# RWKV keys and scan preparation as one block, with the second direction in buffers of its own

## What is computed

```
    def decay(w0, wl, w2):
        logw = -jax.nn.softplus(-(w0 + jnp.tanh(wl) @ w2)) - 0.5
        return jnp.exp(-jnp.exp(logw))
...
    w = jnp.stack([decay(w0_f, wl_f, w2_f), decay(w0_b, wl_b, w2_b)])
    a = jax.nn.sigmoid(jnp.stack([a0_f + al_f @ a2_f, a0_b + al_b @ a2_b]))
    g = jax.nn.sigmoid(gl) @ g2
    kk = heads(k * k_k)
    kk = kk / jnp.maximum(jnp.sqrt(jnp.sum(kk * kk, axis=-1, keepdims=True)), 1e-12)
    k_dir = k * (1.0 + (a - 1.0) * k_a)
    b = kk * heads(a)
```

## Time and profile before

| what | value |
|---|---|
| median of 3 runs | 2814.98 us |
| the three runs | 2815.46, 2814.98, 2808.55 us |
| the profiled execution, its own time | 2809.21 us |
| its span | 2807.4 us |
| keys block, by the timeline | 241.3 to 256.3 us |
| preparation block | 256.6 to 314.2 us |
| first matmul of the scan | 314.50 us |

### The profile page before, as it was taken

One profiled execution on the slowest core, in us unless ns is written; L12 is line 12 of the kernel. 1 busy time (PEld: TensorE's weight loads), 2 busy tenths in 40 slices (PEclk: granted clock), 3 DMA queues, 4 the chain that ended last, 5 costly groups with the idle time before them and its releaser, 6 DMA issues. The chain is left out here.

```text
span 2807.4 us, 42506 instructions
## 1 busy us (share of the span) xinstructions
PE 2462.6 (88%) x18560; PEld 1513.1 (54%) x18560; DVE 1257.8 (45%) x2118; ACT 592.2 (21%) x861; POOL 153.0 (5%) x112
## 2 busy tenths in 40 slices
PE   8977499978999999899777899898989779989887
PEld 6864499956544555388235644343437464434333
DVE  6776766656322332377567611121128741112113
ACT  4343311123111111153501311010012431101001
POOL 0000000013000000020110300000000030000000
PEclk9987599988999999999778999999999889999999
DMA  6560133143999999632110779999972157999996
GB/s 224 185 212 12 54 101 94 57 183 137 417 416 415 418 416 417 259 104 90 39 45 20 289 297 427 428 427 428 427 275 75 62 209 310 427 426 428 427 427 255
DMA packets 121890, 727.04 MB, mean 259 GB/s; under 512 B 12038, under 2 KB 65542, under 8 KB 84679
## 3 DMA queue, kind: packets, MB, share of 16 engines
q1 hardware_dynamic: 92200, 693.82, 61.0%
q10 hardware_dynamic: 29536, 30.93, 3.3%
HBM read 722.63 MB, written 2.10 MB: 258 GB/s over the span
## 5 line engine op out<-in xcount | busy, mean ns | idle before, releaser
L2080 PE MATMUL ps<-s_ring,s_c_XG 128*64 128x512 f32 x2016 | 471.6, 617 | 76.6 <-DMA s_ring<-in_exp_w 62.2
L2080 PEld LDWEIGHTS ps<-s_ring,s_c_XG 128*64 128x64 f32 x2016 | 158.8, 141 | 373.6 <-issue 342.4
L2194 DVE TENSOR_TENSOR s_c_hid<-ps,s_c_sil 128x512 f32<-128x512 f32 x32 | 34.3, 1072 | 507.9 <-PE ps L2080 507.9
L2121 PE MATMUL ps<-s_ring,s_c_hidT 128*64 128x512 f32 x1024 | 223.3, 594 | 0.0
L2080 PE MATMUL ps<-s_ring,s_m_XG 128*64 128x512 f32 x1024 | 222.9, 593 | 0.0
L2080 PEld LDWEIGHTS ps<-s_ring,s_m_XG 128*64 128x64 f32 x1024 | 72.8, 137 | 142.7 <-issue 141.6
L2121 PEld LDWEIGHTS ps<-s_ring,s_c_hidT 128*64 128x64 f32 x1024 | 72.2, 137 | 137.2 <-issue 136.8
L371 PE MATMUL ps<-s_src_part,s_w_hi_at 128*128 128x512 f32 x384 | 124.3, 406 | 0.6 <-DVE s_src_part L1589 0.6
L2206 DVE SCALAR_TENSOR_TENSOR s_c_Y_lo<-ps,s_c_w_slot,s_c_Y_hi 128x512 fp32r<-128x512 f32 x32 | 22.5, 746 | 211.5 <-ACT s_c_Y_hi L2163 211.5
L2121 PE MATMUL ps<-s_ring,s_m_hidT 128*64 128x512 f32 x512 | 113.4, 595 | 0.0
L371 PE MATMUL ps<-s_h_part,s_w_hi 128*128 128x512 f32 x336 | 104.0, 391 | 1.7 <-DVE s_w_lo L349 1.6
(11 more groups left out here) (630 smaller groups left out, 4414.2 us busy)
## 6 DMA issues: line engine op xcount, KB each, us to landing
s_ring<-in_exp_w SPq DMA_DIRECT2D x190, 2048.0 KB, 17.3
s_ring<-in_moe_w_gate SPq DMA_DIRECT2D x32, 2048.0 KB, 12.1
s_ring<-in_moe_w_up SPq DMA_DIRECT2D x32, 2048.0 KB, 14.8
s_ring<-in_moe_w_down SPq DMA_DIRECT2D x32, 2048.0 KB, 12.2
s_mod_w_at<-in_vectors SPq DMA_DIRECT2D x64, 512.0 KB, 4.3
s_mod_w<-in_vectors SPq DMA_DIRECT2D x48, 512.0 KB, 4.6
s_w_raw<-in_w_in ACTq DMA_DIRECT2D x13, 1024.0 KB, 7.2
s_w_raw_at<-in_w_in ACTq DMA_DIRECT2D x8, 1024.0 KB, 5.0
```

The lines of the kernel that those rows point to most:

```text
L2080: last = nc.tensor.matmul(ps[x * SLOTS:(x + 1) * SLOTS, bank + fh, :], XG[:, k, c0:c0 + SLOTS], columns(w[x], at), start=(k == 0), stop=(k ...
L2121: last = nc.tensor.matmul(ps[rows, DOWN + half, :], hidT[:, f, rows], columns(w[x], at), start=(f == 0), stop=(f == nj - 1))
L2194: nc.vector.tensor_tensor(hid_out[:, fh * per:(fh + 1) * per, :], ps[:, UP + fh, :].rearrange("s (p j) -> s p j", j=nj), sil[:, fh * 512:( ...
```

## The change

Both functions go, and one takes their place, with one block: `rwkv_inputs`. The scan's buffers are allocated before it, because it borrows from them: the squares lie in the backward half of the scan's `k` (`sq = kt[:, 1]`), the backward sigmoids in `spare` (the first four tiles of `mix`, which hold GLA's work no longer and RWKV's output not yet), the backward running sum in `v_back`, the backward `a_` in the backward half of `q`. `ex` is still shared by both directions. Each step has a semaphore count of its own (`Since`).

```diff
-        def rwkv_keys(proj, kk, w2, a2, g2, lnk):
...
-        def rwkv_prepare(proj, kk, w2, a2, kd_sum, bufs, reset):
+        def rwkv_inputs(proj, kk, w2, a2, g2, kd_sum, bufs, spare, reset):
...
+            sq = kt[:, 1]
...
+                sgs, ccs, as_, kds = (sg, spare), (cc, v_back), (a_, qt[:, 1]), (kd_sum, kd2)
...
                     @block.tensor
...
+                        for c in range(CT):
+                            head_sums(c)
+                        pe.wait_ge(*here.at(64))
+                        pe.wait_ge(*tanh_done.at(1))
+                        for c in range(CT):
+                            low_w(0, c)
+                        for c in range(CT):
+                            pe.wait_ge(*sig_done.at(c + 1))
+                            low_a(0, c, 4 + c)
+                        pe.wait_ge(*inverted.at(1))
+                        for c in range(CT):
+                            r = slice(32 * c, 32 * c + 32)
+                            nc.tensor.matmul(ps[:, c, :], spread[r, :], sq[r, 1, :], start=True, stop=True).then_inc(*spreaded.up())
+                        for c in range(CT):
+                            pe.wait_ge(*sig_done.at(CT + c + 1))
+                            low_w(1, c)
+                        for c in range(CT):
+                            pe.wait_ge(*scaled_keys.at(c + 1))
+                            low_a(1, c, c)
...
                     @block.scalar
...
+                        def decays(d):
+                            act.wait_ge(*scanned.at(d + 1))
+                            if d:
+                                act.wait_ge(*ex_read.at(1))
...
+                        nc.scalar.activation(proj[:, 12, :], proj[:, 12, :], ACT.Tanh).then_inc(*tanh_done.up())
+                        act.wait_ge(*summed.at(CT))
+                        nc.scalar.activation(sq[:, 0, :], ps[:, 0, :], ACT.Sqrt).then_inc(*rooted.up())
+                        sigmoids(0, 0)
+                        sigmoids(0, 1)
+                        nc.scalar.activation(proj[:, 14, :], proj[:, 14, :], ACT.Sigmoid)
+                        gains(0)
+                        sigmoids(1, 0)
+                        sigmoids(1, 1)
+                        decays(0)
+                        gains(1)
+                        decays(1)
+                        act.wait_ge(*exped.at(4 + TOT))
+                        act.wait_ge(*decayed.at(2))
+                        nc.scalar.activation(v_back[:, :, ::-1], v_[:, :, :], ACT.Copy)
...
                     @block.vector
...
+                        V.reciprocal(sq[:, 1, :], sq[:, 0, :]).then_inc(*inverted.up())
+                        scan(0)
+                        less_own(0)
+                        for c in range(CT):
+                            dve.wait_ge(*spreaded.at(c + 1))
+                            V.tensor_tensor(kk[:, c, :], kk[:, c, :], ps[:, c, :], ALU.mult).then_inc(*scaled_keys.up())
+                        keys(0)
+                        scan(1)
+                        dve.wait_ge(*scaled_keys.at(CT))
+                        gated(0)
+                        products(0)
+                        less_own(1)
+                        keys(1)
+                        gated(1)
+                        products(1)
+                        vlink(V.tensor_tensor(flat(kd_sum), flat(kd_sum), flat(kd2), ALU.add))
...
-                    rwkv_keys(proj, kk, w2, a2, g2, None)
...
-                        rwkv_prepare(proj, kk, w2, a2, kd_sum, bufs, masks["reset"])
+                        rwkv_inputs(proj, kk, w2, a2, g2, kd_sum, bufs, mix[:, 0:CT, :], masks["reset"])
```

More of the change, by code:

```diff
@@ L765, in rwkv_prepare, with _ @@
                 keep = sbuf(st, "rw_keep", [P, CT])
-                m0, a0, v0 = mm_done.n, act_out.n, dve_out.n
-                PER_ACT, PER_DVE = 2 * CT + 6, 4
+                sgs, ccs, as_, kds = (sg, spare), (cc, v_back), (a_, qt[:, 1]), (kd_sum, kd2)
+                EX, SG, CC, TOT = 1, 2, 3, 4
                 with nc.Block() as block:
+                    @block.sync
+                    def _(sp):
+                        for to, name in ((w2[0:64, :], "rw_w2_f"), (w2[64:128, :], "rw_w2_b"), (a2[0:64, :], "rw_a2_f"), (a2[64:128, :], "rw_a2_b")):
+                            sp.dma_start(to, A[name]).then_inc(*here.up(16))
+                        sp.dma_start(g2[:], A["rw_g2"]).then_inc(*gate_here.up(16))
+                        sp.wait_ge(*here.at(64))
+                        sp.wait_ge(*gate_here.at(16))
@@ L769, in _, with head_sums, low_w @@
                     @block.tensor
                     def _(pe):
-                        for d in range(2):
+                        def head_sums(c):
+                            pe.wait_ge(*squared.at(c + 1))
+                            nc.tensor.matmul(ps[32 * c:32 * c + 32, 0, :], head_ones[:, 0:P:4], sq[:, c, :], start=True, stop=True).then_inc(*summed.up())
+                        def low_w(d, c):
                             rows = slice(64 * d, 64 * d + 64)
-                            for j in range(2 * CT):
-                                if d == 1:
-                                    pe.wait_ge(act_out.sem, a0 + j + 1)
-                                c, w, x = j % CT, (w2, a2)[j // CT], proj[rows, 12 + j // CT, :]
-                                nc.tensor.matmul(ps[:, j, :], w[rows, c * P:(c + 1) * P], x, start=True, stop=True).then_inc(*mm_done.up())
+                            nc.tensor.matmul(ps[:, 4 + c, :], w2[rows, c * P:(c + 1) * P], proj[rows, 12, :], start=True, stop=True).then_inc(*low_done.up())
@@ new lines, in low_a @@
+                        def low_a(d, c, bank):
+                            rows = slice(64 * d, 64 * d + 64)
+                            nc.tensor.matmul(ps[:, bank, :], a2[rows, c * P:(c + 1) * P], proj[rows, 13, :], start=True, stop=True).then_inc(*low_done.up())
+                        for c in range(CT):
[4 more added lines that the diff above has]
+                            low_w(0, c)
@@ new lines, in sigmoids, with gains @@
+                        def sigmoids(d, which):
+                            for c in range(CT):
+                                n = (2 * d + which) * CT + c
+                                bank = c if d and which else 4 + c
+                                act.wait_ge(*low_done.at(n + 1))
+                                nc.scalar.activation((sgs, as_)[which][d][:, c, :], ps[:, bank, :], ACT.Sigmoid, bias=vcol((w0_at, a0_at)[which][d], c)).then_inc(*sig_done.up())
+                        def gains(d):
+                            act.wait_ge(*kept.at(1))
+                            act.wait_ge(*sig_done.at((2 * d + 2) * CT))
+                            for c in range(CT):
+                                ins = nc.scalar.activation(kds[d][:, c, :], as_[d][:, c, :], ACT.Identity, bias=keep[:, c:c + 1], scale=vcol("rw_k_a", c))
+                            ins.then_inc(*kd_done.up())
@@ L810, in _, with scan @@
                         V = nc.vector
[L811 to L822 removed]
+                        def scan(d):
@@ new lines, in _ @@
+                        for c in range(CT):
+                            vlink(V.tensor_scalar(kk[:, c, :], k_[:, c, :], vcol("rw_k_k", c), None, ALU.mult))
+                            V.tensor_tensor(sq[:, c, :], kk[:, c, :], kk[:, c, :], ALU.mult).then_inc(*squared.up())
+                        V.tensor_scalar(keep[:], vcol("rw_k_a", 0, CT), -1.0, 1.0, ALU.mult, ALU.add).then_inc(*kept.up())
+                        dve.wait_ge(*rooted.at(1))
+                        vlink(V.tensor_scalar(sq[:, 0, :], sq[:, 0, :], 1e-12, None, ALU.max))
```

129 lines of the change are left out of this document (35 added, 94 removed).

## The result

The changed kernel takes 2794.13 us (median of 7 runs, 2791.45 to 2800.88); before took 2807.24 (7 runs, 2805.41 to 2815.46). The ratio is 0.9942, 95% interval 0.9928 to 0.9956: 0.58% less, 16 us, between 12 and 20; the two medians themselves lie 13.1 us apart (0.47%), so the size of the saving is known to a few us only. All ratios here leave out executions in the chip's slower state (one of e1's ten, 2970.66 us, and one of before beside it, 5045.3 us). The profiled execution has a span of 2792.3 us against 2807.4, 15.1 less. The prediction said 2798 within 2791 to 2808.

What follows compares the result with a forecast made beforehand. DVE was taken to bound the 73 us between GLA and the scan: 13.3 us of waits, plus 0.3 for `keep`, minus 0.3 for new waits, plus 0.2 for gaps, 13.5. 2812.0 less 13.5 gave 2798, range 2791 to 2808.

Steps and rivals of the forecast that it cites:

- How the numbers follow: Whole kernel: 13.5 us saved, taken from the level of before, gives 2798; this forecast had chance 0.79.
- the level of before: Whole kernel's time before the change: 2812.0 us, the middle of the two groups among three runs.
- What bounds: Between GLA and the scan: DVE is the fullest engine, busy 57.01 of 73.00 us; each microsecond removed moves all that follows.
- The waits that go: DVE's waits for spreading, block edge, sigmoids, scans, gain and backward sigmoid: 2.16 + 0.30 + 2.62 + 1.44 + 6.12 + 0.68 = 13.3 us.
- The root: Head of the block: DVE's 1.95 us wait for the root stays, since root and head sums are where they were.
- The total of the stretch: Between GLA and the scan: 13.5 us less, the new block ending near 300.7.
- the new waits: DVE waiting on its own instruction three times (running sum, `ex_read` twice): about 0.1 us each, 0.3 in all.
- TensorE's rate: Low-rank products after the head sums: full rate taken for the forward ones, 0.86 us a product; clock near 1.00 until about 256.
- the last tenth: First exponential, backward products at half rate: ready at 270.2, DVE asking at 270.3, in time by a tenth.
- the first rival: PE stays at half rate: DVE idle 4.3 us for spreading, perhaps 6.0 for `ex`; saving 9.2 or 3.2; chance 0.13.
- The second rival: The scan pays: a cold chunk costs up to 10.9 us more; kernel slower by 8.3 at two chunks; chance 0.05.
- From stretch to whole time: Whole kernel: the stretch's 13.5 us saving taken in full from 2812.0, giving 2798.

Runs made afterwards that it cites:

- e1: Changed kernel with one block kept but the old order on every engine and one set of buffers for both directions: stretch 71.2 us, ratio 1.0004.
- e2: Changed kernel with the backward direction using the forward one's buffers again, the front's order kept: stretch 60.3 us, ratio 0.9963.
- e3: Changed kernel with the first products held back until the reciprocal is complete, TensorE idle meanwhile: stretch 75.2 us, ratio 0.9998.
- e4: Changed kernel with the first products held back likewise, the gap filled with unread matmuls of 128 rows: stretch 61.5 us, ratio 0.9957.
- e12: Changed kernel with the four weightings by r moved into the scan's block and eight warming matmuls before it: 2791.21 us, ratio 0.9934.
- e9: The changed kernel itself run once more, against other runs of before: 2793.13 us, ratio 0.9943, stretch 58.8 us.
- e8: Changed kernel with DVE's last two steps offloaded, seven warming matmuls before the scan and five in its first gap: 2790.59 us, ratio 0.9926.
- e5: Changed kernel with key sum and r weighting moved from VectorE to GpSimd and ScalarE, backward r product first: stretch 63.0 us, ratio 0.9964.
- the bridge: Five unread matmuls after the scan's second job, added to the changed kernel with eleven warming ones before the scan: 2793.06 us, ratio 0.9926.
- e11: Changed kernel with the four weightings by r moved into the scan's block as VectorE's first instructions: 2792.38 us, ratio 0.9939.

## Why the prediction was right, and where it was not

The mechanism held. The step that failed is a term of the sum under "How the numbers follow": the level of before, taken as 2812.0 us from three runs, from which the saving is subtracted. Seven runs have a median of 2807.24, 4.8 less. The bullets take the terms in turn.

- **What bounds.** Right. DVE's list with its waits was the length of the two blocks, and it is the list, with the root's wait, now.
- **The waits that go.** Right one by one. e1 and e2 show that the order of the front carries the gain (10.9 us), and e3 and e4 that it does so only at the full clock. That it is DVE's scaling and norm work, laid into the wait for the gain, is read from the rows; PE's and ACT's new order came with it, and no run parts them.
- **The root.** Mis-sized. "The 1.95 us ahead of it stay": they became 2.51. The head sums took 5.25 us instead of 4.60, because in the kernel before the clock came up under the last of them (0.81 in 246 to 247) and in this execution only behind them (0.50 until 248). In e1 to e12, which have the same head, the wait was 2.16 to 2.57. Of the kernel before there is one trace, so whether its 1.95 was luck stays open.
- **The total of the stretch.** 13.78 against 13.5 is in part luck. Up to the root the stretch grew by 0.65 us (5.90 to 6.55). From the reciprocal's start to the end it shrank by 14.43 (65.87 to 51.44), 0.9 more than forecast: 0.6 because steps were laid end to end at their full durations, though each starts up to 0.1 before the end of the one ahead, and the rest behind the first product, where the new waits cost next to nothing and not 0.3.
- **TensorE's rate.** Right, and more so than said: 1.00 until 263.6, where the prediction looked for it until about 256 and allowed for half rate under the last products, so the exponential was ready at 267.8, three us before it was asked for, and not at the last tenth. e3 is the first rival made real, with waits of 4.56 and 6.44 where 4.3 and 6.0 were written.
- **The second rival's price.** Too high. 10.9 us a cold chunk compared a chunk with waits of its own with one without; with the clock held up by the bridge the first chunk was 2 to 5 shorter. The scan did take 2.8 us more in this kernel's profiled execution, in its later part and not in the first chunk. Whether the change has a share in that is not shown: the changed kernel has 262.4 and 261.4 (e9), before 259.6 in its one trace, and e2, with the same front, 257.6.
- **From stretch to whole time.** This is the failed step. With the measured 2807.2 in place of 2812.0 the sum gives 2793.7, and 2794.1 was measured. But the other executions of before have medians of 2808.80, 2809.99 and 2811.59, nearer to what was assumed, and by the ratio the saving is 16 us, not 13.5. So how much of the centre's miss of 4 us is the level, and how much a saving outside the stretch, stays open; the ratio's interval holds the 13.8 of the stretch (0.9951), and no second cause is shown.

## What to carry to other kernels

Look in a stretch bounded by one engine for long waits that could be filled with work queued just ahead of or behind them; here a new order of the front on three engines was worth eleven microseconds, and joining the blocks under two. When the order lets another engine run at the rate it had before, check what rate it will have: in e3 the same products took twice as long after an idle gap. A warm-up has to reach up to the work: e8's ended 11 us too early. Before handing work to GpSimd, see whether VectorE reads two SBUF operands at that time; a wait in the next block can be the better place.

## What the runs showed of the hardware

- Matmuls on 64 of the rows, with eight on 32 among them, did not raise TensorE's clock in 29.80 us without a gap (e3, 0.50), and did not let it fall in the changed kernel either (1.00 over 248.2 to 263.6); in the kernel before it rose after forward and backward products had run side by side. Under or right behind the head sums, which use 128 rows and 32 columns, it rose each time (before 0.81 in 246 to 247, changed 0.98 in 248 to 249).
- Beside GpSimd's addition a VectorE product with both inputs in SBUF took 6.58 us instead of 2.29 and ended 2.1 us after the addition (e5). Beside GpSimd's memsets four VectorE instructions kept their 2.74 us (e11).
- Code that was not edited varied by 8 us in the scan (254.9 to 263.3) and by 8 behind it (2228.8 to 2236.9), more than half of what the change gained.
